# Key selection of a sparse attention layer: counts of the widest tile one projection later, masks written by ScalarE

## The reference

```
logits = einsum("bthd,bsd->bths", qib, k_idx)
score = einsum("bth,bths->bts", wb, relu(logits))
score = where(causal, score, -inf)
_, sel = top_k(score, topk)          # topk = 256; ties go to the lower index
```

## Time and profile before

| | us |
|---|---|
| median of 3 runs | 2611.58 (2609.6 to 2612.11) |
| the profiled execution | 2611.07 |
| its span, first to last instruction | 2609.4 |
| the selection in the span | 1257 to 1532 |
| VectorE busy of the span | 1598.0 (61%) |
| TensorE busy of the span | 2410.7 (92%) |

### The profile page before, as it was taken

How to read it: one execution, slowest core, us unless ns; L and a number is a source line. 1 busy time by engine, 2 the same in 40 slices (tenths; PEclk the granted TensorE clock), 3 DMA queues, 4 the chain that set the end, 5 groups by cost and what they waited for, 6 DMA issues and landing times. The chain is left out here.

```text
span 2609.4 us, 49274 instructions
## 1 busy us (share of the span) xinstructions
PE 2410.7 (92%) x19407; PEld 1250.0 (48%) x19407; DVE 1598.0 (61%) x2638; ACT 1128.4 (43%) x1817; POOL 789.7 (30%) x911
## 2 busy tenths in 40 slices
PE   5999996899799997799999988889999999999999
PEld 3555644455455554345444434344444544544544
DVE  7787776222222223666599999636757747847863
ACT  6110454232223333655656558414734724815720
POOL 2012021433333332342454422001612702603502
PEclk9999997999999999899999999899999999999999
DMA  8677657899999998320112249632001020020133
GB/s 252 185 268 234 242 165 291 294 408 409 408 409 376 407 408 324 104 65 25 45 37 97 97 112 189 209 114 81 9 33 73 9 75 31 9 97 17 66 121 129
DMA packets 213403, 451.70 MB, mean 173 GB/s; under 512 B 112225, under 2 KB 122337, under 8 KB 204769
## 3 DMA queue, kind: packets, MB, share of 16 engines
q1 hardware_dynamic: 171360, 368.02, 39.6%
q0 software_dynamic: 22768, 43.14, 5.1%
q10 hardware_dynamic: 19088, 37.91, 4.1%
HBM read 371.07 MB, written 58.94 MB: 165 GB/s over the span
## 5 line engine op out<-in xcount | busy, mean ns | idle before, releaser
L2905 POOL TENSOR_TENSOR group_words<-group_words 128x1024 f16<-128x1024 f16 x64 | 153.9, 2427 | 377.3 <-PE i_pj L146 368.1
L1600 PE MATMUL m_gu<-arena,m_xT 128*32 128x256 f32 x2880 | 231.2, 386 | 6.6 <-DMA arena<-in_moe_w_up 6.6
L1685 DVE TENSOR_TENSOR m_xT<-m_xm,row_gain 128x256 f32<-128x256 f32 x89 | 38.0, 427 | 306.9 <-PE m_gu L1600 306.8
L144 PE MATMUL i_pj<-hT,group_words 128*128 128x512 f16 x384 | 146.2, 381 | 13.6 <-DVE group_words L368 8.2
L1600 PEld LDWEIGHTS m_gu<-arena,m_xT 128*32 128x32 f32 x2880 | 117.3, 111 | 65.3 <-issue 15.5
L1655 ACT ACTIVATE m_sg<-m_gu 64x256 f32<-64x256 f32 x88 | 33.6, 382 | 261.9 <-PE m_gu L1600 261.9
L145 PE MATMUL i_pj<-hT,group_words 128*128 128x512 f16 x384 | 146.3, 381 | 0.0
L144 PE MATMUL s_pj<-hT,arena 128*128 128x512 f16 x368 | 141.2, 384 | 5.5 <-issue 5.4
L146 PE MATMUL i_pj<-hT,group_words 128*128 128x512 f16 x384 | 146.1, 380 | 0.0
L145 PE MATMUL s_pj<-hT,arena 128*128 128x512 f16 x368 | 140.8, 383 | 0.0
L146 PE MATMUL s_pj<-hT,arena 128*128 128x512 f16 x368 | 140.7, 382 | 0.0
(11 more groups left out here) (657 smaller groups left out, 6625.0 us busy)
## 6 DMA issues: line engine op xcount, KB each, us to landing
arena<-in_moe_w_down SPq DMA_DIRECT2D x17, 2048.0 KB, 26.4
arena<-in_moe_w_up SPq DMA_DIRECT2D x16, 2048.0 KB, 23.1
arena<-in_moe_w_gate SPq DMA_DIRECT2D x16, 2048.0 KB, 25.4
x_tok<-in_ada_w ACTq DMA_DIRECT2D x8, 2048.0 KB, 11.9
conv_y<-in_moe_w_gate SPq DMA_DIRECT2D x7, 2048.0 KB, 29.2
conv_y<-in_moe_w_up SPq DMA_DIRECT2D x7, 2048.0 KB, 16.4
hT<-in_moe_w_gate SPq DMA_DIRECT2D x6, 2048.0 KB, 26.7
hT<-in_moe_w_up SPq DMA_DIRECT2D x6, 2048.0 KB, 20.2
```

The source lines that it names most:

```text
L144: nc.tensor.matmul(out, lhsT=lh, rhs=rh, start=start, stop=False)
L1600: last = nc.tensor.matmul(gu_ps[tile(j), 0:FFN // 2], lhsT=xT[:, c % 2, c // 2, :], rhs=expert_unit(k, e, part)[:, c, halves[i]], start=c ...
L1685: nc.vector.tensor_tensor(xT[:, :, :, :], xm[:, :, :, :], of_rows(shift), ALU.add).then_inc(xt_sb, 1)
L2905: return tuple(k.nc.gpsimd.tensor_tensor(k.y_U[:, t % 2, n], k.adt_parts[:, n, t, heads].unsqueeze(2).to_broadcast([P, HPG, P]), k.upto16. ...
```

## The change

Three things are edited. `sums_by` allots the sums about one projection later: sum 0 alone stands ahead of the emptying of 7, sums 1 to 3 ahead of 8, and the last two ahead of 21. For tiles 0 to 4 VectorE no longer writes the mask: it writes the flags over the tile's scores and raises `chosen`. And ScalarE writes these five masks (`to_bias`, flag times 1e30 minus 1e30), two ahead of the emptying of projection 6 and three at the very end of its program. The widest tile's mask stays on VectorE.

```diff
--- before.py
+++ after.py
@@ -2318,9 +2318,10 @@
         k.gates_stored, k.gates_stores = stored, 16 * (n_jobs - early) // 2
         part_high, part_low = k.sem("s_part_high"), k.sem("s_part_low")
         first_part = len(blocks)
+        chosen = k.sem("s_chosen")
         compared, summed, widest = k.sem("s_compared"), k.sem("s_summed"), len(blocks) - 1
         at_least, rounds = sb("at_least", [P, S], BF16), 33
-        sums_by = lambda j: min(rounds, max(0, (9 * (j - 5)) // 4))
+        sums_by = lambda j: min(rounds, max(0, (9 * (j - 6) - 2) // 4))
         groups = [range(0, 2), range(2, 6)]
         share = [range(i - 1, i) if i else () for i in range(len(blocks) - 1)] + [range(len(blocks) - 2, n_jobs)]
         block = ctx.enter_context(nc.Block())
@@ -2389,6 +2390,11 @@
                     act.wait_ge(pj_done, j - 1)
                 act.wait_ge(scaled, j + 1)
                 nc.scalar.copy(ws[:, 0, j % 2], w[:, j % 2]).then_inc(high, 1)
+
+            def to_bias(i):
+                n, at = causal(blocks[i])
+                act.wait_ge(chosen, i + 1)
+                nc.scalar.activation(k.bias[:, at:at + n], work[:, work_at[i]:work_at[i + 1]], ACT.Copy, bias=-BIG, scale=BIG)
 
             def sums(a, e):
                 for n in range(a, e):
@@ -2417,6 +2423,9 @@
                     if share[i][0] < j < n_jobs - 1:
                         split(j + 1)
                     sums(sums_by(j - 1), sums_by(j))
+                    if j == first_part:
+                        for n in groups[0]:
+                            to_bias(n)
                     act.wait_ge(pj_done, j + 1)
                     if j >= early + 2:
                         act.wait_ge(stored[j % 2], 16 * ((j - early) // 2))
@@ -2427,6 +2436,8 @@
                         act.wait_ge(*((part_low, n - 1) if n >= 2 else (used, len(blocks) * (IDX_HEADS - 1))))
                         nc.scalar.copy(k.parts[n][:, 0, :], k.whole[n]).then_inc(part_high, 1)
             sums(sums_by(n_jobs - 1), rounds)
+            for n in groups[1][:-1]:
+                to_bias(n)
 
         @block.gpsimd
         def _(pool):
@@ -2520,8 +2531,13 @@
                     step(v.tensor_scalar(e, scores(i), least(i), None, ALU.is_equal))
                     step(v.tensor_tensor_scan(r, e, e, 0.0, ALU.add, ALU.max))
                     step(v.scalar_tensor_tensor(e, in0=r, scalar=room[:, i:i + 1], in1=e, op0=ALU.is_le, op1=ALU.mult))
-                    step(v.scalar_tensor_tensor(e, in0=scores(i), scalar=least(i), in1=e, op0=ALU.is_gt, op1=ALU.add))
-                    step(v.tensor_scalar(k.bias[:, at:at + n], e, -1.0, BIG, ALU.add, ALU.mult))
+                    if i < widest:
+                        v.scalar_tensor_tensor(scores(i), in0=scores(i), scalar=least(i), in1=e, op0=ALU.is_gt,
+                                               op1=ALU.add).then_inc(chosen, 1)
+                        dve.wait_ge(chosen, i + 1)
+                    else:
+                        step(v.scalar_tensor_tensor(e, in0=scores(i), scalar=least(i), in1=e, op0=ALU.is_gt, op1=ALU.add))
+                        step(v.tensor_scalar(k.bias[:, at:at + n], e, -1.0, BIG, ALU.add, ALU.mult))
 
 
 BRANCH_READY = 2
```

## The result

The changed kernel took 2614.68 us (median of 20 runs, 2610.85 to 2619.1) against 2610.0 (20 runs, 2604.96 to 2614.19): ratio 1.0016, 95% interval 1.001 to 1.0023, which is 2.6 to 6.0 us slower. It was forecast at 2613.8, 2.2 us over before. The profiled execution took 2617.77 us, with a span of 2616.1.

A forecast was written before the change was run, and what follows sets the result against it. VectorE was taken to bound the selection's end, TensorE 0.8 us behind. Compare 32 4.2 us later, less 2.6 at the end, gave 1.6; plus 0.6 for attention, 2.2 over before: 2613.8 us, range 2612.5 to 2615.5 (chance 0.5).

The forecast's parts named there:

- VectorE bounds, TensorE's gap is ScalarE's doing: Selection: VectorE ends last by 0.8 us; TensorE's 4.39 us idle ahead of projection 8 comes from ScalarE's late emptying 6.
- Masks: Masks leaving VectorE: compare 0 comes 0.86 us earlier, and 2.1 us go at the selection's end.
- Stalls: First two rounds: VectorE waits 2.3 us for sum 0 and 3.5 us for sum 1, then nothing further.
- Slow hand-overs: VectorE's hand-overs beside GpSimd's subtractions, 1.35 us each: 16.9 us before, 17.5 us taken after the change.
- rival 1: First four rounds: stalls mostly absorbed or four or more slow hand-overs shed; -3.0 us, 2608.6 us; chance 0.12.
- Attention's start: First attention products run at TensorE's low clock after some 10 us of idle: 0.6 us more, bounds 0 and 2.
- The sum: Whole kernel: selection 1.6 us longer plus attention 0.6, so 2.2 us over before, 2613.8 us.
- Rival 2: Selection's end: TensorE keeps its hold ahead of projection 8, ScalarE's late masks end the stage; +1.7 us, 2613.3; chance 0.06.
- Rival 3: Projections 10 to 20: VectorE's stalls recur, about 0.4 us each, 4.4 us beside the 2.2; 2618.2 us; chance 0.15.

The follow-up runs named there:

- e2: Kernel before with only the later allotment of sums, all masks left on VectorE; ratio 1.0018, 5.0 us over before.
- e1: Changed kernel with the old allotment of sums, so only the masks moved to ScalarE; ratio 1.0004, 0.9 us over before.
- e4: The changed kernel run again with no edit; ratio 1.0007, 2.4 us over before.
- e11: Changed kernel with 48 unread products keeping TensorE busy at the end of the stage; ratio 1.0013, 2.4 us over before.
- e3: Changed kernel with sums allotted between the old and new schedules, (9 * (j - 6) + 4) // 4; ratio 0.9996, 1.4 us under before.
- e8: e3 with the three late masks moved ahead of emptying 22; ratio 1.0009, 1.0 us over before.
- e7: e1 with the three late masks moved ahead of emptying 22; ratio 0.9995, 1.3 us under before.
- e5: Changed kernel with 7 sums allotted for three projections and the three late masks ahead of emptying 22; ratio 0.9995, 1.8 us under before.
- e9: The kernel of e5 run again; ratio 0.9994, 1.9 us under before.
- e12: e8 with 22 unread products keeping TensorE busy at the end of the stage; ratio 0.9994, 2.0 us under before.

## Why the prediction was right

- **VectorE bounds, TensorE's gap is ScalarE's doing.** Right. Projection 8's gap went, as forecast, with the late allotment alone (e2: 0.8 us of gaps left) and not with the masks alone (e1: 5.4). The last emptying, forecast for 1521.5 to 1524, came at 1526.20, of which 1.8 us are the later start of the stage and 1.6 the later end of projection 0.
- **Masks.** Right that the wait for `chosen` adds nothing. The masks took ScalarE 0.52, 0.63 and 0.95 us at 384, 512 and 896 keys; 0.7 and 1.0 were taken from the nearest rows. The gain at the end was 1512.76 to 1536.66, 23.9 us, against 26.9 before: 3.0, where the sum had 2.6. It is split otherwise than forecast: with the late allotment alone the end took 25.7 (e2), with the masks alone 25.1 (e1), so the masks gave 1.8 for 2.1 and the shift of GpSimd's work 1.2 for 0.5. The 0.86 us ahead of compare 0 were saved too, and brought nothing, as e2 shows.
- **Stalls.** The two places and their cause were right, and that nothing follows them. The sizes were 3.03 and 5.12 us in this trace, 8.1 for 5.8; in e4 they were 2.4 and 4.0, in e11 the same, 6.4 in all. Yet what the stalls lead to was forecast exactly: compare 2 was to come at 1373.1, 93.4 us behind the end of projection 0, and it came 93.3 behind it in all three traces of the changed kernel. The stalls are only the rest of VectorE's time up to there. In e4 and e11 they are 0.6 longer than forecast mainly because VectorE got to its wait for sum 1 sooner: its hand-over after sum 0 took 1.3 us, for which the sum had 1.97, taken from a later one with an operation more. In the first trace they are another 1.7 longer because VectorE came to compare 0 sooner: 74.7 us behind the end of projection 0, where it came 76.4 behind it in the other eleven traces with the masks on ScalarE (77.3 in the two with them on VectorE). Why that one execution differs is not shown; by itself it cost no time, since compare 2 stood where it does in e4.

The 1.6 us by which this trace's selection is longer still are TensorE's clock at the start of the stage:

```profile
1257.00:1280.00 23.00, 21.24 (x66) 7.97 (x68) 4.89 (x21) 13.29 (x21) 14.13 (x23) 0.78 0.26 92
```

```profile
1259.00:1283.00 24.00, 22.24 (x64) 8.05 (x62) 6.04 (x26) 13.02 (x20) 13.90 (x23) 0.72 0.25 88
```

It was 0.78 in the first 23 us before and 0.72 in the first 24 after. Before, four products of projection 0 were at 1.2 GHz, after it eleven, so that it ended 1.6 us later. This is no effect of the change: e3 had eleven as well, e8 ten, e4 and e11 four, and in e3 and e8 compare 0 came later by as much as projection 0 ended later, so that everything behind it moved along.

- **Slow hand-overs.** I took 17.5 us. Rounds less 129.9 less waits give 16.8 before, 16.9 after, and 15.6 to 16.9 in all the other kernels: the subtractions of GpSimd cost the same within one slow hand-over (1.35 us) wherever they fall, and neither a drift upwards nor rival 1's shedding of four of them occurred. All but 1.3 us of the difference between kernels' rounds is waits.
- **Attention's start.** 0.6 us taken, bounds 0 and 2. Up to the fifth mask it was 0.3 us in the first trace and -0.3 in e4; e11 gives no more than 2. The size can't be told from zero. The step that was wrong is the comparison: the low clock was already there before, behind only 2.40 us of idle. The second product of the attention before:

```profile
1532.73 0.54 PE L145 MATMUL a_s<-x_tok 128*128 128x512 f16 x1
```

Nine of its first ten products ran at 1.2 GHz; in the changed kernel it was ten, in e4 seven.
- **The sum.** Forecast for the selection +1.6 us; measured +2.9 and +1.7 in two traces, and behind the end of projection 0 +1.3, +1.0 and, in e11, +1.3. That is close, and a little of it is luck: against e11 the sum had 0.6 too little for the stalls and 0.6 too much for the slow hand-overs, which cancel, and 0.4 too little for the gain at the end. With 0.6 for the attention the forecast was a ratio of 1.0008. The interval of e4 holds it; that of the first measurement begins just above it, at 1.001; the 4.7 us lie within the 5.2 that the prediction took for no difference that can be measured, but 20 runs of each did tell them from none, where e4's 11 did not. The stalls do not explain this, since the selection lost less than forecast; where the rest of the first measurement's 4.7 us lies is open, and its profiled execution can't tell, being 3.1 us above the median. That the time itself came within 0.9 us of 2613.8 is luck in part: the forecast was put on a median of three runs, 2611.58, which over 20 runs is 2610.0.
- **Rivals.** Rival 2 (ScalarE's masks end the stage) did not occur in the change, since TensorE gained, but is exactly what e1 showed. Rival 3 (stalls recur) did not: all waits lie in the first two rounds.

## What to carry to other kernels

When an engine serves two masters in a fixed order, the order is a phase: here, shifting one master's requests by a whole step moved the wait to the other, and of the three places tried the one between was the best for the stage. Write the allotment as a rate and an offset and sweep the offset: here the wait of 4.4 us for TensorE ahead of projection 8 and the 6.4 to 8.1 in all for VectorE became 0.2 and 1.6 in e3, between them, and the stage behind projection 0 3.6 us shorter than before. The time did not follow clear of its scatter. Before crediting work taken off the engine that ends a stage, look at who comes 0.8 us behind it, and at where the work is queued instead: e1 gave its whole 2.5 us back by placing it behind the last emptying, and e7 kept some, 0.6 us of the stage, by using a wait that was there. And before reading a stage's length from one trace, look for a point inside it behind which repeats agree: from the end of projection 0 on they did within 0.4 us, over the whole stage only within 1.2.

## What the runs showed of the hardware

- A short idle time is not free for TensorE's clock. After 2.43 us of idle e5's first five products came 0.22 us apart and the sixth took 0.63; after the same 2.43 us in e9, the same kernel, already the first took 0.58. After 1.86 us (e7) and 0.50 us (e12) they stayed at 2.4 GHz. Unread products in the idle time cost nothing on the path and made the attention 127.5 to 128.4 us long, against 129.1 to 133.1 in all others but e7 (1.9 us idle, 127.2).
- The same program's TensorE clock in the first 23 us of a stage differed between executions (0.78 and 0.72), worth 1.6 us of TensorE time: over the 14 traces three to eleven products of projection 0 took longer than 0.5 us.
- The activation table load was issued ahead of the wait of its activation and ran inside it: 1.28 us at 1364.02, then 3.96 us of waiting. It took no time of the path.
- Four-column operations on VectorE took 0.17 us with GpSimd quiet and, two of the three in a hand-over, 0.59 and 0.70 beside its subtractions; with a compare of 1.06 for 0.75 this made a round 5.4 us instead of 4.06. The counting operations did not change (0.87 us at 640 columns in both). That cost was 15.6 to 16.9 us in every allotment.
- VectorE and TensorE kept a fixed distance over rounds that do not wait for each other: compare 0 came 76.4 us behind the end of projection 0 (77.3 with the early masks on VectorE) in 13 of 14 traces, whether that end was 22.6 or 24.2 us into the stage, and 74.7 in one. Through what, and why not in that one, is not shown.
